# RWKV-7 scan norms by block-ones products with Ln and Exp, squares summed in pairs, and last weight chunks tile by tile, in a two-block transformer kernel on one core

## The chip, the cores and the metric

One core of one Trainium2 chip (trn2). The metric is the device time of one execution in microseconds (us); the time of a kernel is the median of several executions. TensorE, VectorE, ScalarE, GpSimd and SyncE run programs of their own and wait for each other by semaphores.

## The reference

256 tokens of width 2048 in fp32 go through two blocks. The first is an RWKV-7 mixer and a convolutional FFN, both with an adaptive modulation; the second is windowed attention beside HGRN2, and an MLP. Before and behind each of the four halves stands an RMS norm over all 2048 channels. What matters here, cut from the reference:

```python
def _rms(x, g):
    return x * lax.rsqrt(jnp.mean(x * x, axis=-1, keepdims=True) + 1e-6) * g
...
kk = heads(k * k_k)                       # 32 heads of 64 channels
kk = kk * lax.rsqrt(jnp.maximum(jnp.sum(kk * kk, axis=-1, keepdims=True), 1e-24))
...
y = _rwkv7_scan(rh, heads(decay), kh, vh, -kk, kk * ah)
mean = jnp.mean(y, axis=-1, keepdims=True)
var = jnp.mean(jnp.square(y - mean), axis=-1, keepdims=True)
y = (y - mean) * lax.rsqrt(var + 64e-5)
...
x = x + g_m * _rms(y, norm_mix_post)
h = _rms(x, norm_ffn_pre) * (1 + sc_f) + sh_f
f = _conv_ffn(h, ffn_w_in, ffn_conv_w, ffn_conv_b, ffn_w_out)
x = x + g_f * _rms(f, norm_ffn_post)
...
h = rmsnorm(x, mix_pre_gain_2)            # second block
x = x + rmsnorm(mixed, mix_post_gain_2)
x = x + rmsnorm(mlp(rmsnorm(x, mlp_pre_gain_2)), mlp_post_gain_2)
```

## The kernel before

**Layout.** Activations lie transposed: 16 tiles of 128 channels by 256 tokens. SyncE loads each weight in chunks (four k-tiles of 128 rows by up to 512 columns; the FFN's second product has chunks of two k-tiles) into a ring of raw slots. ScalarE copies a chunk into WH (L1208), VectorE subtracts that from the raw chunk into WL (L1715), three slots each, and both do so in the order of a fixed list of chunks; `walk(n)` brings an engine's part of that list up to chunk n. Activations are split into a high and a low half in the same way (XB). A product of a k-tile and an output tile is two matmuls: L779 over 512 columns (WH with both halves of the activations), L781 over 256 (WL with the high half).

**gemm() of TensorE (L760 to L790)** takes the output in groups of four tiles, each in a PSUM bank, and a group's weights chunk by chunk. In a chunk the k-tile is the outer loop and the output tile the inner one, so a group's four tiles end together behind the last k-tile of the last chunk. Each ended tile counts `s_tile`; ScalarE copies it out of the bank (L1270), or VectorE adds it to what is there (L1769, L1771), VectorE adds the low columns (L1762) and counts `s_ev`. `hook` calls other work in between.

**The RMS norms** have names: x and f before the first block's halves, o and f2 behind them, p, m, o2, m2 the same for the second block, at for attention's output. ScalarE squares a tile (`square`, L1211 to L1215, `s_sq`) into XX, a ring of three slots. TensorE adds it into bank 7 with a matmul by a 128x128 matrix of ones (`stat`, L741 to L748, `s_sqmm`), one matmul for each of 16 tiles. ScalarE takes the root (`root`, L1217 to L1220), VectorE the reciprocal (L1727 to L1729). For o, f2, o2 and m2 the squares of a group are made and summed beside the next group's chunks, two hooks a chunk; the last group's four come in `residual` (ScalarE L1240 to L1243) behind the gemm: for tiles 12 to 15 a square and a copy times the gain each, then the root. For p and m, whose norm is applied behind the product, a sum stands ahead of each k-tile of the first group. GpSimd does nothing in these stages but a few loads.

**prenorm("f")** (ScalarE L1295, VectorE L1856) makes the FFN's 16 input tiles: VectorE times the reciprocal root, ScalarE the modulation and the high half (into XB), VectorE the low half. The weight chunks whose slots are not free before are split behind it.

**The scan (447 to 878 us)** does the 32 heads in eight blocks of four heads (512 columns: four chunks of 64 tokens by two pairs of heads by 64). A round r holds `stage_t` of block r (six levels of 64x64 products on TensorE: L903, L913, L918, each followed by VectorE's TS L1986, WS L1979, QS L1990), `stage_s` of block r-1 (the state from chunk to chunk, TensorE L939 to L973, ScalarE's RS L1384, VectorE's UV L2005), and `side(r)`: the preparation of block b = r+1 and the end of block e = r-2. The three are generators, woven step by step by hand in the same order in each engine's program; where one engine waits, all steps behind stand too. `side` of all engines uses two PSUM banks, 6 and 7, in the order of the list ROUND (L526), a bank coming free when its READER (L528) has read it. In rounds 2, 4, 6, 8 a sixteen-instruction product of the modulation vector (L848) is in between, and VectorE accumulates other parts of it with L1698.

**The norms in side().** The keys' squares (kp) go through `head_sums` (L798: four matmuls with two columns of block ones each, giving 8 sums a token row), VectorE's maximum with 1e-24 into NS [128, 8], ScalarE's Sqrt (L1346), VectorE's reciprocal (L1899), `over_heads` (L803 to L809: eight matmuls of a broadcast column with the identity, spreading a value over its head's 64 rows; 16 instructions in the trace) and VectorE's product with kk (L1917). The output's squares (Y2) go the same way: VS, Sqrt (L1350), reciprocal (L1920), `over_heads`, product with y (L1941).

## Time and profile before

| | |
|---|---|
| median of the runs | 2953.48 us (3 runs, 2941.91 to 2957.41) |
| profiled execution | 2959.37 us, its span 2957.5 us |
| mean granted TensorE clock of the core | 0.963 of full speed |
| scan | 446.84 to 878 us; rounds 0 to 8 start at 446.84, 486.13, 528.21, 585.67, 634.34, 691.72, 740.39, 793.87, 832.67 |
| TensorE, weight load, VectorE, ScalarE, GpSimd busy | 95%, 80%, 63%, 43%, 3% |

A busy share is an average over the span. Engines in rows: PE is TensorE's matmul, PEld its weight load, DVE VectorE, ACT ScalarE, POOL GpSimd. In a timeline row the first number is the start in us from the span's start, the second the duration; in brackets stands the idle time of the engine before the instruction and what ended it. In a stretch the columns are its ends and length, the busy time (and count) of PE, PEld, DVE, ACT and POOL, the granted clock, the busy share of the DMA engines and their GB/s. A function table load of ScalarE is the row ACT_TABLE_LOAD.

### The profile page before, as it was taken

Reading aid. Unit: us, or ns where it says so; the run is one execution under the profiler, and the core shown is the slowest. Engines: PE = TensorE matmul, PEld = TensorE weight load, DVE = VectorE, ACT = ScalarE, POOL = GpSimd, SP = SyncE. Lnnn points to the kernel's source line nnn. Section 1 sums busy time; section 2 is a strip of 40 time slices with the busy share of each in tenths; the row PEclk is TensorE's granted clock in tenths of the full one; section 3 lists DMA queues with packets and bytes.
Section 4 is the critical chain, followed back from the end, with each engine's and each line's share of the span. In section 5 each row is a group of like instructions: output and inputs, shape, how many; then the busy total and the mean of one; then the engine's idle time right before and its main releaser. Section 6 shows DMA issues by size and latency. Waiting matters only on the chain.

```text
span 2957.5 us, 45793 instructions
## 1 busy us (share of the span) xinstructions
PE 2801.5 (95%) x19618; PEld 2374.6 (80%) x19618; DVE 1863.2 (63%) x2460; ACT 1281.7 (43%) x1735; POOL 102.6 (3%) x127
## 2 busy tenths in 40 slices
PE   6999988989879899999999989999999999999997
PEld 2488877778768688888888878888978888888886
DVE  3787647667644676766776756567656556565655
ACT  1244433332214555445445545466554444343443
POOL 0121001111000000000000000000000000000000
PEclk9999988889879899999999999999999999999999
DMA  9767732222316364866676545543445555555552
GB/s 385 260 233 238 255 125 80 101 86 83 105 58 207 107 192 148 294 199 196 236 243 194 172 156 163 170 144 100 132 139 181 189 185 179 191 185 182 186 189 85
DMA packets 289210, 514.11 MB, mean 174 GB/s; under 512 B 10096, under 2 KB 122736, under 8 KB 288880
## 3 DMA queue, kind: packets, MB, share of 16 engines
q1 hardware_dynamic: 286016, 500.21, 50.5%
q0 software_dynamic: 2560, 7.90, 0.8%
q8 instruction: 155, 2.54, 0.4%
q10 hardware_dynamic: 432, 3.07, 0.3%
q14 instruction: 47, 0.39, 0.0%
HBM read 508.91 MB, written 2.10 MB: 173 GB/s over the span
## 4 chain that ended last, share of the span: by engine, by line
PE 86%; DVE 5%; ACT 4%; issue 2%; DMA 2%; DVEq 0%; SPq 0%; POOL 0%; ACTq 0%
PE ps L779 46%; PE ps L781 23%; PE ps L745 2%; PE ps L918 2%; DMA RAWa<-in_ada_w 1%; PE ps L913 1%; PE ps L688 1%; PE ps L903 1%; PE ps L806 1%; ACT WHb L1208 1%; PE ps L1065 1%; PE ps L870 1%; PE ps L969 1%; PE ps L800 1%; PE ps L880 1%
## 5 line engine op out<-in xcount | busy, mean ns | idle before, releaser
L779 PE MATMUL ps<-XB,WHb 128*128 128x512 f32 x2304 | 833.6, 405 | 22.6 <-DVE WLb L1715 17.0
L781 PE MATMUL ps<-XB,WLb 128*128 128x256 f32 x2304 | 649.0, 282 | 0.0
L1715 DVE TENSOR_TENSOR WLb<-RAWb,WHb 128x2048 fp32r<-128x2048 f32 (+1 forms) x196 | 426.7, 2192 | 274.5 <-ACT WHb L1208 274.0
L779 PEld LDWEIGHTS ps<-XB,WHb 128*128 128x128 f32 x2304 | 437.0, 190 | 130.7 <-issue 18.3
L1208 ACT ACTIVATE WHb<-RAWb 128x2048 fp32r<-128x2048 f32 (+1 forms) x196 | 356.7, 1832 | 315.8 <-PE ps L781 279.4
L1715 DVE TENSOR_TENSOR WLd<-RAWd,WHd 128x2048 fp32r<-128x2048 f32 x144 | 328.2, 2289 | 253.2 <-ACT WHd L1208 253.2
L779 PE MATMUL ps<-XD,WHd 128*128 128x512 f32 x1280 | 460.0, 402 | 0.0
L781 PEld LDWEIGHTS ps<-XB,WLb 128*128 128x128 f32 x2304 | 439.3, 191 | 1.2
L1208 ACT ACTIVATE WHd<-RAWd 128x2048 fp32r<-128x2048 f32 x144 | 274.7, 1916 | 354.6 <-PE ps L781 354.6
L779 PE MATMUL ps<-FB,WHd 128*128 128x512 f32 x1024 | 364.5, 399 | 0.0
L781 PE MATMUL ps<-XD,WLd 128*128 128x256 f32 x1280 | 360.3, 281 | 0.0
L779 PEld LDWEIGHTS ps<-XD,WHd 128*128 128x128 f32 x1280 | 241.2, 188 | 59.1 <-DVE XD L1851 0.3
L781 PE MATMUL ps<-FB,WLd 128*128 128x256 f32 x1024 | 287.8, 281 | 0.0
L779 PE MATMUL ps<-XA,WHa 128*128 128x512 f32 x768 | 270.6, 398 | 1.7 <-DVE R L1762 1.7
L779 PE MATMUL ps<-FA,WHb 128*128 128x512 f32 x688 | 245.2, 401 | 0.4 <-DVE R L1762 0.4
L781 PEld LDWEIGHTS ps<-XD,WLd 128*128 128x128 f32 x1280 | 240.9, 188 | 0.7
L779 PEld LDWEIGHTS ps<-FB,WHd 128*128 128x128 f32 x1024 | 192.5, 188 | 47.4
L781 PE MATMUL ps<-XA,WLa 128*128 128x256 f32 x768 | 214.2, 279 | 0.0
L781 PE MATMUL ps<-FA,WLb 128*128 128x256 f32 x688 | 193.1, 281 | 0.0
L781 PEld LDWEIGHTS ps<-FB,WLd 128*128 128x128 f32 x1024 | 192.2, 188 | 0.3
L779 PEld LDWEIGHTS ps<-XA,WHa 128*128 128x128 f32 x768 | 144.2, 188 | 36.4 <-DVE R L1762 2.0
L779 PEld LDWEIGHTS ps<-FA,WHb 128*128 128x128 f32 x688 | 129.2, 188 | 32.2 <-DVE R L1762 0.7
(335 smaller groups left out, 3510.6 us busy)
## 6 DMA issues: line engine op xcount, KB each, us to landing
RAWb<-in_ffn_w_in SPq DMA_DIRECT2D x168, 512.0 KB, 5.1
RAWd<-in_w_up SPq DMA_DIRECT2D x64, 1024.0 KB, 5.2
RAWd<-in_w_down SPq DMA_DIRECT2D x64, 1024.0 KB, 5.1
RAWa<-in_ada_w SPq DMA_DIRECT2D x48, 1024.0 KB, 7.4
RAWa<-in_rwkv_w_rkv SPq DMA_DIRECT2D x48, 1024.0 KB, 5.6
RAWb<-in_ffn_w_out SPq DMA_DIRECT2D x36, 1024.0 KB, 5.5
RAWs<-in_ada_w SPq DMA_DIRECT2D x32, 1024.0 KB, 5.0
RAWb<-in_w_in SPq DMA_DIRECT2D x44, 512.0 KB, 5.0
```

The lines of the kernel that those rows point to most:

```text
L688: mm = pe.matmul(banks[ROW_BANKS[piece % 2][m]][0:1, :], SC[:, 2 * kc + 1:2 * kc + 2], RAW["a"][:, slot_of[i], 1024 + m * 512:1536 + m * 5 ...
L745: pe.matmul(banks[7][:, 0:T], ones, XX[:, (xx_at[stage] + j) % 3, :], start=(j == 0), stop=(j == n - 1), skip_group_check=True).then_inc(s ...
L779: pe.matmul(bank[:, :], WH[tag][:, w, o:o + P], acts(k), start=(k == 0), stop=False)
L781: mm = pe.matmul(bank[:, 0:T], WL[tag][:, w, o:o + P], acts(k)[:, 0:T], start=False, stop=last)
L800: mm = pe.matmul(bank[:, 2 * k:2 * k + 2], squares[:, k * P:(k + 1) * P], head2, start=True, stop=True)
L806: mm = pe.matmul(bank[64 * h:64 * h + 64, k * P:(k + 1) * P], rows[:, 2 * k + h:2 * k + h + 1].to_broadcast([P, 64]), ident, start=True, s ...
L870: mm = pe.matmul(bank[h][:, m * P:(m + 1) * P], BK[o, 4 * gg + m, :], AR[o, 4 * gg + m, :], start=True, stop=True)
L880: mm = pe.matmul(bank[:, i * T:(i + 1) * T], G2[:, k, i * P:(i + 1) * P], SG[:, k, :], start=(k == 0), stop=(k == 1))
L903: mm = pe.matmul(pair_at(pair_wt, m, u0), GM[rows, gm_index(m, u0), 0:64], istack[rows, :] if lv == 0 else TS[rows, m, :], start=True, sto ...
L918: mm = pe.matmul(pair_at(pair_q, m, u0), WS[rows, m, :], istack[rows, :] if lv == 0 else QS[rows, m, :], start=True, stop=True)
L1208: act.activation(WH[tag][:, n % WN, 0:size], RAW[tag][:, slot_of[i], 0:size], ACT.Copy).then_inc(s_wh, 1)
L1715: dve.tensor_tensor(WL[tag][:, n % WN, 0:size], RAW[tag][:, slot, 0:size], WH[tag][:, n % WN, 0:size].bitcast(F32), ALU.subtract).then_inc ...
```

## The change

1. Scan. Both norms' sums are one matmul over 512 columns with the 128x128 block ones (`blk`), which leaves in each row the sum of its head. For the keys VectorE takes the maximum with 1e-24 over 512 columns into sig, ScalarE Ln and then Exp with scale -0.5 (the inverse root), VectorE the product with kk. For the output ScalarE reads the bank with Ln (scale 1/64, bias a new constant eps_head), then Exp, VectorE the product with y. `head_sums`, `over_heads`, NS, VS, the two reciprocals and their steps and banks go. The maximum stands a step later in VectorE's order than before.
2. GpSimd adds the squares of two tiles (`pair_sums`), and `stat` is called for pairs: for tiles 0 to 11 in o, f2, o2, m2 and for all 16 in p, m.
3. In each gemm the last chunk of groups 1 and up has the output tile as the outer loop. ScalarE's `evac_to` makes squares of tiles 12 to 14 between its copies for o and o2; `residual` makes the squares first, then the root, then the four gain copies.
4. prenorm("f") calls `walk` for two weight chunks inside its loop: ScalarE ahead of tiles 8 and 12, VectorE behind tiles 10 and 14.

The diff, cut to its core:

```diff
-ROUND = [("a", "z"), ("a", "a"), ("e", "m1"), ("a", "n"), ("e", "v"), ("a", "nb"), ("p", "w"), ("e", "vb"), ("a", "bt0"),
+ROUND = [("a", "z"), ("a", "a"), ("e", "m1"), ("a", "n"), ("e", "v"), ("p", "w"), ("a", "bt0"),
          ("a", "bt1"), ("a", "g0"), ("a", "g1"), ("a", "g2"), ("a", "g3"), ("e", "g"), ("a", "bb"),
          ("a", "bv")]
-READER = {"z": (aA, "s1"), "a": (aA, "a1"), "n": (aV, "max"), "nb": (aV, "kkn"), "bt0": (aA, "bkt0"),
+READER = {"z": (aA, "s1"), "a": (aA, "a1"), "n": (aV, "max"), "bt0": (aA, "bkt0"),
           "bt1": (aA, "bkt1"), "g0": (aV, "gm0"), "g1": (aV, "gm1"), "g2": (aV, "gm2"), "g3": (aV, "gm3"),
-          "bb": (aV, "bo"), "bv": (aA, "uv1"), "m1": (zV, "mean"), "v": (zV, "var"), "vb": (zV, "nrm"),
+          "bb": (aV, "bo"), "bv": (aA, "uv1"), "m1": (zV, "mean"), "v": (zA, "lg"),
           "g": (zV, "out")}
...
-        pe.wait_ge(s_sq, sq_at[stage] + j + 1)
+        if j < n_pair[stage]:
+            pe.wait_ge(s_sp, pair_at_[stage] + j // 2 + 1)
+        else:
+            pe.wait_ge(s_sq, sq_at[stage] + j + 1)
         pe.matmul(banks[7][:, 0:T], ones, XX[:, (xx_at[stage] + j) % 3, :], start=(j == 0),
-                  stop=(j == n - 1), skip_group_check=True).then_inc(s_sqmm, 1)
-        if j == n - 1:
+                  stop=(j >= n - 2 if j < n_pair[stage] else j == n - 1),
+                  skip_group_check=True).then_inc(s_sqmm, 1)
+        if square_done(stage, j)[1] == sum_end[stage]:
             last7[0] = (s_rt, rms_no[stage] + 1)
...
-            if g and half:
-                stat(stage, 4 * g - 4 + ci, ND)
+            if g and half and ci % 2:
+                stat(stage, 4 * g - 5 + ci, ND)
...
-                for kk_, k in enumerate(ch["ks"]):
-                    if g == 0:
-                        if stage:
-                            stat(stage, k, ND)
-                        pe.wait_ge(*ready(k))
+
+                def product(kk_, k, t):
+                    i = gm.base[g] + t
+                    if k == 0 and tile_before[i] is not None:
+                        pe.wait_ge(s_ev, tile_before[i] + 1)
+                    o = kk_ * width + t * P
+                    bank = banks[tile_bank[i]]
+                    pe.matmul(bank[:, :], WH[tag][:, w, o:o + P], acts(k), start=(k == 0), stop=False)
+                    last = k == chunks[-1]["ks"][-1]
+                    mm = pe.matmul(bank[:, 0:T], WL[tag][:, w, o:o + P], acts(k)[:, 0:T],
+                                   start=False, stop=last)
+                    if last:
+                        mm.then_inc(s_tile, 1)
+                    return mm
+
+                full = len(ch["ks"]) == 4
+                if g and ch is chunks[-1]:
                     for t in range(nt):
-                        i = gm.base[g] + t
-                        if k == 0 and tile_before[i] is not None:
-                            pe.wait_ge(s_ev, tile_before[i] + 1)
-                        o = kk_ * width + t * P
-                        bank = banks[tile_bank[i]]
-                        pe.matmul(bank[:, :], WH[tag][:, w, o:o + P], acts(k), start=(k == 0), stop=False)
-                        last = k == chunks[-1]["ks"][-1]
-                        mm = pe.matmul(bank[:, 0:T], WL[tag][:, w, o:o + P], acts(k)[:, 0:T],
-                                       start=False, stop=last)
-                        if last:
-                            mm.then_inc(s_tile, 1)
-                    if hook and kk_ == 1 and len(ch["ks"]) == 4:
-                        hook(g, ci, 0)
+                        for kk_, k in enumerate(ch["ks"]):
+                            mm = product(kk_, k, t)
+                        if hook and t == nt // 2 - 1 and full:
+                            hook(g, ci, 0)
+                else:
+                    for kk_, k in enumerate(ch["ks"]):
+                        if g == 0:
+                            if stage and k % 2:
+                                stat(stage, k - 1, ND)
+                            pe.wait_ge(*ready(k))
+                        for t in range(nt):
+                            mm = product(kk_, k, t)
+                        if hook and kk_ == 1 and full:
+                            hook(g, ci, 0)
...
             pe.wait_ge(*aA(b, "sq"))
-            head_sums(take("a", b, "n"), kp[:, :]).then_inc(aP.sem, 1)
+            pe.matmul(take("a", b, "n")[:, :], blk, kp[:, :], start=True, stop=True).then_inc(aP.sem, 1)
...
             pe.wait_ge(*zA(e, "sq"))
-            head_sums(take("e", e, "v"), Y2).then_inc(zP.sem, 1)
-        if b is not None:
-            pe.wait_ge(*aV(b, "rec"))
-            over_heads(take("a", b, "nb"), NS).then_inc(aP.sem, 1)
+            pe.matmul(take("e", e, "v")[:, :], blk, Y2, start=True, stop=True).then_inc(zP.sem, 1)
         yield
...
-    def residual(stage, gm, n_pg):
+    def square_of(stage, gm, j):
+        act.wait_ge(s_ev, gm.tile0 + j + 1)
+        square(stage, j, R[:, j, :])
+
+    def residual(stage, gm, first):
+        for j in range(first, ND):
+            square_of(stage, gm, j)
+        root(stage)
         for j in range(12, ND):
-            squared(stage, gm, j, n_pg)
-        root(stage)
+            act.activation(R[:, j, :], R[:, j, :], ACT.Copy, scale=GB[:, j:j + 1]).then_inc(s_rs, 1)
...
-    def evac_to(dst):
+    def evac_to(dst, stage=None):
         def evac(gm, g):
             for t in range(n_tiles(gm, g)):
                 i = gm.base[g] + t
                 act.wait_ge(s_tile, i + 1)
                 act.activation(dst(gm, g, t), banks[tile_bank[i]][:, 0:T], ACT.Copy).then_inc(s_evh, 1)
+                if stage and g == 3 and t:
+                    square_of(stage, gm, 4 * g + t - 1)
...
-    def prenorm(stage, dst, scale, bias):
+    def prenorm(stage, dst, scale, bias, first):
         for j in range(ND):
+            if j in (8, 12):
+                walk(first + j // 4)
...
             act.wait_ge(*aV(b, "max"))
-            act.activation(NS[:, :], NS[:, :], ACT.Sqrt).then_inc(aA.sem, 1)
+            act.activation(sig[:, :], sig[:, :], ACT.Ln).then_inc(aA.sem, 1)
+            act.wait_ge(*aA(b, "lg"))
+            act.activation(sig[:, :], sig[:, :], ACT.Exp, scale=-0.5).then_inc(aA.sem, 1)
         yield
         if e is not None:
-            act.wait_ge(*zV(e, "var"))
-            act.activation(VS[:, :], VS[:, :], ACT.Sqrt).then_inc(zA.sem, 1)
+            act.wait_ge(*zP(e, "v"))
+            act.activation(Y2, e_bank(e, "v")[:, :], ACT.Ln, scale=1.0 / 64, bias=cst("eps_head")).then_inc(
+                zA.sem, 1)
+            act.wait_ge(*zA(e, "lg"))
+            act.activation(Y2, Y2, ACT.Exp, scale=-0.5).then_inc(zA.sem, 1)
         yield
...
             if j > 1:
                 lo(j - 2)
+            if j in (10, 14):
+                walk(first + j // 4)
...
-            dve.wait_ge(*aP(b, "n"))
-            dve.tensor_scalar(NS[:, :], a_bank(b, "n")[:, 0:8], 1e-24, None, ALU.max).then_inc(aV.sem, 1)
         yield
         if b is not None:
-            dve.wait_ge(*aA(b, "rt"))
-            dve.reciprocal(NS[:, :], NS[:, :]).then_inc(aV.sem, 1)
-        if e is not None:
-            dve.wait_ge(*zP(e, "v"))
-            dve.tensor_scalar(VS[:, :], e_bank(e, "v")[:, 0:8], 1.0 / 64, 64e-5, ALU.mult,
-                              ALU.add).then_inc(zV.sem, 1)
-        if b is not None:
+            dve.wait_ge(*aP(b, "n"))
+            dve.wait_ge(*aG(b, "pm"))
+            dve.tensor_scalar(sig[:, :], a_bank(b, "n")[:, :], 1e-24, None, ALU.max).then_inc(aV.sem, 1)
...
         if b is not None:
-            dve.wait_ge(*aP(b, "nb"))
-            dve.tensor_tensor(kk[:, :], kk[:, :], a_bank(b, "nb")[:, :], ALU.mult).then_inc(aV.sem, 1)
-        if e is not None:
-            dve.wait_ge(*zA(e, "rt"))
-            dve.reciprocal(VS[:, :], VS[:, :]).then_inc(zV.sem, 1)
+            dve.wait_ge(*aA(b, "rs"))
+            dve.tensor_tensor(kk[:, :], kk[:, :], sig[:, :], ALU.mult).then_inc(aV.sem, 1)
...
         if e is not None:
-            dve.wait_ge(*zP(e, "vb"))
-            dve.tensor_tensor(y, y, e_bank(e, "vb")[:, :], ALU.mult).then_inc(zV.sem, 1)
+            dve.wait_ge(*zA(e, "rs"))
+            dve.tensor_tensor(y, y, Y2, ALU.mult).then_inc(zV.sem, 1)
...
+    def pair_sums(stage):
+        for j in range(0, n_pair[stage], 2):
+            u = xx_at[stage] + j
+            pool.wait_ge(s_sq, sq_at[stage] + j + 2)
+            pool.tensor_tensor(XX[:, u % 3, :], XX[:, u % 3, :], XX[:, (u + 1) % 3, :],
+                               ALU.add).then_inc(s_sp, 1)
+
...
     pool.memset(UT[:, :, 0:2], 0.0).then_inc(s_utz, 1)
+    for stage in ("o", "f2", "p"):
+        pair_sums(stage)
     pool.wait_ge(s_xn, 2 * ND)
...
     pool.wait_ge(s_kd, 32)
+    for stage in ("o2", "m", "m2"):
+        pair_sums(stage)
```

`square_done(stage, j)` names the semaphore value at which square j has been read (by GpSimd's addition, `s_sp`, for the second of a pair; else by `stat`, `s_sqmm`); the list of XX's free slots is made from it. `n_pair` is 12 for o, f2, o2, m2, 16 for p and m, 0 for x, f, at.

## Rows read from the trace of the kernel before

**Rows 1.** The page's first part: busy time of TensorE, share of the span, instructions
```profile
PE 2801.5 (95%) x19618; PEld 2374.6 (80%) x19618; DVE 1863.2 (63%) x2460; ACT 1281.7 (43%) x1735; POOL 102.6 (3%) x127
```

**Rows 2.** Waits of TensorE's matmuls after the scan: total, times, longest
```profile
PE ps L779 <- DVE WLb L1715: 17.0, 3, 10.3
```

**Rows 3.** Stretches of scan rounds 2, 3 and 6: busy time by engine, granted clock, DMA
```profile
528.21:585.67 57.46, 51.58 (x789) 45.11 (x785) 35.94 (x63) 16.18 (x29) 6.63 (x8) 0.82 0.25 83
585.67:634.34 48.67, 44.31 (x773) 38.60 (x769) 36.34 (x62) 16.08 (x29) 7.71 (x8) 0.93 0.29 98
740.39:793.87 53.48, 47.59 (x788) 41.59 (x785) 35.94 (x63) 16.07 (x29) 5.59 (x6) 0.90 0.26 85
```

**Rows 4.** Timeline of TensorE in round 3: start, duration, [idle before, releaser]
```profile
590.13 1.10 PE L830 MATMUL ps<-MX,C 128*128 128x512 f32 x2 [0.78 <-ACT b L1319]
...
593.68 1.15 PE L903 MATMUL ps<-TS,GM 64*64 64x64 f32 x32
596.68 0.53 PE L963 MATMUL ps<-UV,BKT 128*64 128x64 f32 x8 [1.85 <-DVE UV L2005]
...
599.37 1.97 PE L806 MATMUL ps<-C,NS 128*64 128x128 f32 x16
...
605.43 1.15 PE L903 MATMUL ps<-TS,GM 64*64 64x64 f32 x32
...
609.46 1.15 PE L913 MATMUL ps<-WS,QS 64*64 64x64 f32 x32 [1.39 <-DVE WS L1979]
```

**Rows 5.** Timeline of ScalarE in round 3
```profile
591.99 0.63 ACT L1330 ACTIVATE XX<-MX 128x512 f32<-128x512 f32 x1 [0.87 <-DVE MX L1885]
...
596.67 1.28 ACT L1346 ACT_TABLE_LOAD   x1
```

**Rows 6.** Timeline of VectorE in round 3
```profile
600.32 0.68 DVE L1979 TENSOR_TENSOR WS<-ps,C 128x512 f32<-128x512 f32 x1
...
601.85 0.68 DVE L1917 TENSOR_TENSOR b<-b,ps 128x512 f32<-128x512 f32 x1
...
602.56 1.24 DVE L1698 SCALAR_TENSOR_TENSOR ACCs<-RAWs,SC,ACCs 128x1024 f32<-128x1024 f32 x1
```

**Rows 7.** The same work (level 2 to level 3) in rounds 2 and 6, as stretches
```profile
556.68:566.54 9.86, 9.86 (x125) 8.76 (x125) 5.06 (x10) 1.66 (x3) 0.00 (x0) 0.52 0.01 2
768.98:774.74 5.76, 5.76 (x125) 5.12 (x125) 5.06 (x10) 1.56 (x3) 0.00 (x0) 1.00 0.02 3
```

**Rows 8.** Timeline of ScalarE where it loads function tables, ahead of the scan
```profile
171.65 1.28 ACT L1284 ACT_TABLE_LOAD   x1
...
173.33 1.28 ACT L1285 ACT_TABLE_LOAD   x1
```

**Rows 9.** Chain of waits in the output projection: start, duration, one sum each
```profile
973.19 0.43 PE ps L745 x2
...
979.17 0.43 PE ps L745 x2
```

**Rows 10.** GpSimd's 128x256 adds: duration min, median, max
```profile
L2360 POOL TENSOR_TENSOR XX<-HV x48: 607/722/1594, 72.8 to 300.5; 128x256 f32<-128x256 f32 x48
```

**Rows 11.** Timeline of TensorE in the second block's input projection, first group
```profile
1774.72 0.59 PE L745 MATMUL ps<-XX,C 128*128 128x256 f32 x2
...
1776.55 0.59 PE L745 MATMUL ps<-XX,C 128*128 128x256 f32 x2
```

**Rows 12.** Timeline of TensorE where the FFN waits for a weight chunk
```profile
1025.95 0.50 PE L779 MATMUL ps<-XB,WHb 128*128 128x512 f32 x1 [4.05 <-DVE WLb L1715]
```

**Rows 13.** The stretch behind that wait: busy time, granted clock
```profile
1025.95:1031.30 5.35, 5.35 (x21) 4.64 (x22) 4.34 (x2) 1.22 (x1) 0.00 (x0) 0.68 0.81 252
```

**Rows 14.** Timelines of ScalarE at the square roots that end three projections
```profile
988.78 0.47 ACT L1219 ACTIVATE RST<-ps,C 128x256 f32<-128x256 f32 x1 [0.39 <-PE ps L745]
...
1762.27 0.47 ACT L1219 ACTIVATE RST<-ps,C 128x256 f32<-128x256 f32 x1
...
2941.66 0.47 ACT L1219 ACTIVATE RST<-ps,C 128x256 f32<-128x256 f32 x1 [0.39 <-PE ps L745]
```

92 lines of the change are left out of this document (46 added, 46 removed).

## The prediction

> **What bounds the kernel now.** I read the page first: TensorE is busy for 95% of the span [rows 1], so outside its idle stretches only less TensorE work shortens anything. Then the waits of TensorE behind the scan: there are few, and the largest that this change touches is for split weight chunks [rows 2]. Then the scan (447 to 878 us), stretch by stretch: there every round costs 48.7 us (rounds 3, 5), 53.5 (round 6) or 57.4 (rounds 2, 4), and the granted clock goes with it, 0.93, 0.90, 0.82 [rows 3]. One round at close range shows a chain of short steps over four engines [rows 4 to 6]: TensorE computes the level-1 product (L903, 593.68), then idles 1.85 us, and can go on with that level only at 601.0. What it waits for is VectorE's WS (L1979), which starts at 600.32 although its input was there at 594.8: VectorE executes in order, and ahead of WS stand the reciprocal of the keys' norms (waiting for a table load and Sqrt on ScalarE) and the output's sum (waiting for TensorE's eight two-column matmuls). At the end of this stretch TensorE waits again, 1.39 us, for the level-2 WS [rows 4]. Last, the clock: the same work, level 2 to level 3, takes 5.76 us at clock 1.00 and 9.86 us at 0.52 [rows 7], so a fall of the 2.4 GHz clock to 1.2 GHz there costs 4.1 us. It happened in rounds 2 and 4, behind an idle time of 2.06 us and one of 1.39; round 3, with only the 1.39, was spared.
>
> **Scan, keys' norms.** Per round go: 8 two-column instructions (1.05 us), the 16 of L806 (1.97 us at the low clock, [rows 4]), a Sqrt, a max and a reciprocal on 8 columns (0.2 each). Added: one 512-column product, 1.10 us as L830 [rows 4], so nothing is won at the sums themselves; a max over 512 columns, 0.68 as any VectorE operation of that size [rows 6]; Ln and Exp over 512 columns, 0.63 each [rows 5]. And table loads. Now a round has three, at Sigmoid, Exp and Sqrt, 1.28 us each. I count a load for each of Ln, Exp, Ln, Exp, six in a round, because of [rows 8]: Tanh and Sigmoid, one behind the other, each had their own load. The Trainium skill ("ScalarE activation tables", section Table sets in the compiler and the runtime) says that loads are placed by the greedy longest run of functions, and "ScalarE: Activation LUTs" (The hidden batching unit) that one set has both ln and exp and that Tanh is in Sigmoid's set. By that a round would have two loads; the trace, with two loads where that rule gives one, speaks against it.
>
> Replay of round 3 with the rows' durations. ScalarE is done with kp at 596.67 [rows 5]: load 1.28, Ln 0.63, load 1.28, Exp 0.63 give 600.5. VectorE has QS, UV by 595.95 (0.6 earlier, the 8-column max has left the step before), then max 596.6, AR 597.4, WS 598.0 instead of 601.0. TensorE: the state products 596.0 to 596.9, the output's sum to 598.0, level-1 products 598.1 to 600.1, U to 601.1. VectorE: kk 600.6 to 601.2, the accumulation (L1698, 1.24) to 602.5, TS 603.1. Level 2 starts at 603.2, was 605.43. Then QS, AR and two BK to 605.5, the output's product 606.1 (its Ln and Exp end at 604.4), WS 606.7; TensorE's next at 606.8, was 609.46: **2.65 us** earlier. Behind it the order is as before. GpSimd's product of kk waits for kk as before and is no later. RS (L1384) stands behind four ScalarE steps now and comes at 604.8, 0.7 earlier than before: no loss.
>
> In rounds 2, 4, 6 a vector of MOD is added between (L848, sixteen instructions). There level 2's second part starts 28.5 us after the round's start (556.68-528.21, 768.98-740.39, [rows 3, 7]) against 23.8 in round 3. By the replay it is 21.1 for round 3 and 1.1 more with L848 at the full clock: 22.2, **6.3 us** earlier.
>
> **The clock's price.** The replay leaves TensorE idle for 2.1, 0.6 and 1.4 us between 601.1 and 606.8, more than before in round 3, and the one stretch of before that looks like it (round 2) had the fall. So I charge 4.1 us [rows 7] to rounds 3, 5 and 6, which have no long fall now; rounds 2 and 4 have it already. Sum: 2x(2.65-4.1) + 2x6.3 + (6.3-4.1) = 11.9. Rounds 0, 1, 7, 8 have one L806 call each in front of the next product, 2.0 us [rows 4]: 8.0. Together **19.9 us**. Bounds: nothing won (loads eat all of it) and 19.9+20.5 = 40.4 (no fall in the five rounds).
>
> **Pair sums.** A sum over the tiles' squares takes 0.43 us of the path [rows 9]; in the gemms of "o", "f2", "o2", "m2" six each go: 24x0.43 = 10.3. GpSimd's add takes 0.72 (median, up to 1.59, [rows 10]) and lies beside a chunk of 5.98 us [rows 9]. Only f2's short chunks (two k-tiles) are too short for it: I charge 0.4 three times. 9.1. In the first groups of "p" and "m" TensorE is the bound too: 1.83 us from sum to sum [rows 11] is four tiles' products and one sum. Eight of 16 sums go in each: 16x0.43 = 6.9. The ring of three XX slots lets ScalarE run one tile less ahead, but at 1.4 us a step of TensorE that still covers a square (0.4) and an add. If GpSimd's adds take 1.59 each time, "p" and "m" win nothing: 6.9 is the term's bound below.
>
> **Last chunks tile by tile.** Tiles end 1.4 us apart instead of together. Of the tails, "o": the root at 988.78 [rows 14] waits for eight ScalarE operations in a row, of which four gain copies go behind the root, and the squares of tiles 12 to 14 before the end. New: last square at 986.4, the sums (five behind the gemm's end, 985.05) at 987.3: 1.45 us. "o2" is the same, 1.4. "f2" (root 1762.27, ahead of it a table load 1.28, which starts a gain copy and a tile's sum earlier) 1.45, "m2" (2941.66) 1.35, bounded by the five sums. **5.65**. Bound below: 0, when these sums run at the low clock. Between groups TensorE waits for no bank now, and the earlier evictions only help; same matmuls, same number.
>
> **Weight chunks inside "f".** TensorE waits 4.05 us for a chunk that ScalarE copies only behind all 16 prenorm tiles [rows 12], and the clock behind it is 0.68 for 5.35 us [rows 13]: at two levels that is 3.4 us at half, 1.7 lost. Moved ahead of tile 8, the chunk is split by about 1019.7, needed at 1021.9; the tiles behind it come 2 to 5 us later, but TensorE needs one only every 1.39. **5.75**; lower bound 1.7, if tile 12 comes late instead. No transfer starts otherwise: the DMAs of these chunks have landed, and SP's queue gets its slots no later. GpSimd's order changes too: its mask loads stand behind the "p" sums, some 2 us later, and are used a group later.
>
> **Sum.** 9.1+6.9+5.65+5.75 = 27.4 outside the scan, 19.9 in it: 47.3. The profiled execution took 2959.37 (span 2957.5), 5.9 above the median of the runs, 2953.48. So 2912.1 for that execution, and **2906 us** against the median.
>
> **The rivals.** (a) *The second fall stays away*: the 512-column products keep TensorE active. For it: rounds 3 and 5 have one fall only. Against: idle 4.1 of 5.7 us. 20.5 less: 2886. (b) *Fewer table loads*: Ln and Exp find their table loaded, two loads a round in place of six. kk at 597.9 instead of 600.5, 2.6 us less in each of 8 rounds, 20.8: 2885. (It is what the Trainium skill's rule above would give.) (c) *The scan wins nothing*: the four ScalarE operations and loads, 7.7 us a round for both norms, delay RS and the output's product. For it: ScalarE's order puts RS behind them. 2926. (d) *Slower*: in the middle of the round the clock stays low. All of round 3 behind 609.46, 24.9 us, at the factor 9.86/5.76 costs 17.7 us; in rounds 1 to 7 that is 124, less the 20.5 counted: about 3010. It decides above 8.9 us a round, half of that stretch. Against: in no round of before did a fall outlast the 128-column products. (e) *The change doesn't do what it says*: GpSimd becomes the wait of the sums in "p", "m" and the gemms. 16.0 less gain: 2922, which I take together with (c).
>
> **Chances.** Forecast 0.40, (a) 0.18, (b) 0.10, (c) and (e) 0.20, (d) 0.03; the rest, 0.09, lies between (c) and no change, from partly longer falls. One measurement of this kernel tells 0.5%, 14.8 us, from no change: faster 0.88, same 0.08, slower 0.04. Range: down to 2875 (most of (a) and (b)), up to 2938 ((c) and three further falls, 12.3).
>
> **What would show it.** In the profile of after: 0.43 us sums 40 fewer; the chunk wait of 4.05 gone; roots 1.4 earlier after the last product; in a middle round six table loads, kk about 15 us after the round's start; granted clock of rounds 3 and 5 below 0.93, of 6 at 0.82. A prediction of this size is wrong if rounds 3 and 5 are longer than 52 us, or if a round has two loads.

## The result, and the profile after

The kernel after takes **2927.05 us** (median of 7 runs, 2911.74 to 2932.53) against 2954.29 for the kernel before (7 runs, 2941.91 to 2959.64): ratio **0.991**, 95% interval 0.9894 to 0.9927, 27 us faster. Its profiled execution took 2927.05 (span 2925.2, granted clock 0.968), that of before 2959.37 (2957.5, 0.963): 32.3 us between the spans. I forecast 47.3 for the profiled execution and 2906 for the median. The experiments ran on four chips, each beside runs of the kernel before; their ratios are to those runs and compare the versions better than the medians do.

The page's first part, which answers to [rows 1]. TensorE has 45.5 us less to do, ScalarE 45 us more, GpSimd 79 more:

```profile
PE 2756.0 (94%) x19186; PEld 2322.3 (79%) x19186; DVE 1871.6 (64%) x2436; ACT 1326.6 (45%) x1776; POOL 181.8 (6%) x167
```

I read both traces at the same landmarks (the scan's first level-0 product, GpSimd's memory set behind the scan, the square roots of the norms, the first group's copies in the FFN, the first product of the FFN's and of the MLP's last part) and wrote down how the difference grows from each to the next. The last column is a second execution of the kernel after, described below, against the same execution of before:

| stretch | forecast | after | after, again |
|---|---|---|---|
| up to the scan | 0 | -2.3 | -5.0 |
| scan | -19.9 | -27.5 | -26.7 |
| output projection, to the root of o | -4.05 | -3.1 | -2.2 |
| prenorm f, to the first group's end | -5.75 | -6.0 | -6.1 |
| FFN, to its last part | 0 | +3.4 | -2.5 |
| that part, to the root of f2 | -2.85 | **+5.3** | +3.8 |
| to the root of p | -3.45 | **+1.3** | +1.2 |
| attention, HGRN2, to the root of o2 | -4.0 | -2.8 | -2.7 |
| to the root of m and the last part of the MLP | -3.45 | **+2.8** | +2.8 |
| to the root of m2 | -3.95 | -3.5 | -3.5 |

In these traces the scan won more than forecast and everything behind it next to nothing, 2.5 us. Both sizes hold for one pair of executions: against a second execution of the kernel before, described below too, the second one of the kernel after won 20.3 us in the scan and 6.8 behind it. In both pairs f2, p and m lost, and the scan won in other rounds than forecast. So there are two questions: why the middle of the kernel lost, and what won in the scan.

**The stalls in f2.** The list of TensorE's waits behind the scan (total, times, longest) has a new entry, three times 2.2 us for GpSimd's sums. The 4.05 us for a weight chunk of [rows 12] are gone; the two waits that stay under its name are the 13.2 us behind the scan, 10.3 before, and one of 2.6. The 13.2 us are no loss: TensorE's own last product of the scan ends earlier, and its next product starts 9.4 us behind the scan's end, 9.5 before.

```profile
PE ps L795 <- DVE WLb L1744: 15.7, 2, 13.2
PE ps L764 <- POOL XX L2389: 6.6, 3, 2.2
```

The timelines of GpSimd, VectorE and TensorE at the first of the three:

```profile
1676.60 2.53 POOL L2389 TENSOR_TENSOR XX<-XX 128x256 f32<-128x256 f32 x1 [11.11 <-ACT XX L1229]
```
```profile
1676.26 2.29 DVE L1744 TENSOR_TENSOR WLb<-RAWb,WHb 128x2048 fp32r<-128x2048 f32 x1 [0.41 <-ACT WHb L1222]
```
```profile
1679.19 0.70 PE L764 MATMUL ps<-XX,C 128*128 128x256 f32 x2 [2.15 <-POOL XX L2389]
...
1680.43 0.63 PE L795 MATMUL ps<-FA,WHb 128*128 128x512 f32 x1
```

GpSimd's addition has its two squares at 1676.5, but VectorE has begun to subtract a weight chunk 0.3 us earlier. The addition ends 0.6 us behind that subtraction: 2.53 us, where I had 0.72 from [rows 10]. Behind the stall the clock falls too (0.63 us for the 512-column product that takes 0.40 at the full clock). Over all 40 additions:

```profile
L2389 POOL TENSOR_TENSOR XX<-XX x40: 728/2275/2736, 891.7 to 2896.1; 128x256 f32<-128x256 f32 x40
```

**Round 3 of the scan**, which I had replayed. Here are its stretches and those of rounds 7 and 8 (the columns of [rows 3]; round 7 of before first, then after), and rows of TensorE, ScalarE and VectorE in round 3, which begins at 576.58:

```profile
793.87:832.67 38.80, 35.01 (x694) 31.29 (x691) 27.09 (x44) 4.04 (x9) 0.72 (x1) 0.91 0.36 117
832.67:878.81 46.14, 36.68 (x232) 28.69 (x230) 12.51 (x27) 6.59 (x15) 0.72 (x1) 0.63 0.02 6
```
```profile
576.60:624.90 48.30, 42.11 (x727) 35.27 (x725) 36.80 (x59) 22.02 (x34) 8.60 (x8) 0.93 0.30 99
...
778.60:811.81 33.21, 31.35 (x671) 27.17 (x669) 26.97 (x42) 7.68 (x12) 0.72 (x1) 1.00 0.41 137
811.81:849.09 37.28, 27.15 (x188) 18.83 (x186) 11.96 (x23) 13.84 (x21) 0.73 (x2) 0.80 0.03 8
```
```profile
594.98 1.97 PE L917 MATMUL ps<-TS,GM 64*64 64x64 f32 x32 [3.28 <-DVE TS L2008]
...
598.58 1.98 PE L927 MATMUL ps<-WS,QS 64*64 64x64 f32 x32 [0.79 <-DVE WS L2001]
```
```profile
588.54 1.28 ACT L1370 ACT_TABLE_LOAD   x1
...
590.48 1.28 ACT L1372 ACT_TABLE_LOAD   x1
...
592.42 1.28 ACT L1376 ACT_TABLE_LOAD   x1
...
594.42 1.28 ACT L1379 ACT_TABLE_LOAD   x1
```
```profile
592.43 0.69 DVE L1942 TENSOR_TENSOR b<-b 128x512 f32<-128x512 f32 x1 [2.09 <-ACT b L1372]
```

Each of Ln, Exp, Ln, Exp has its own table load, as I took from [rows 8]; the Trainium skill's rule of the greedy longest run ("ScalarE activation tables", Table sets in the compiler and the runtime) does not describe this program. kk's product starts 15.9 us after the round's start (forecast 14.9). Level 2 starts at 18.4 (forecast 17.5, before 19.8 by [rows 4]), behind an idle time of 3.28, and the next product at 22.0 (21.1; 23.8), 1.8 earlier than before. At level 2 the clock falls: 1.97 us for the product that took 1.15. The round ends up 0.4 us shorter. I had named the granted clock as a sign, below 0.93 in rounds 3 and 5 and 0.82 in round 6; it was 0.93, 0.87 and 0.87.

By rounds the scan went like this; the last column has the second execution of each kernel:

| rounds | before | after | forecast | measured | second executions |
|---|---|---|---|---|---|
| 0 and 1 | 39.3, 42.1 | 39.1, 43.5 | -4.0 | +1.2 | +3.6 |
| 2 and 4 | 57.5, 57.4 | 49.4, 51.4 | -12.6 | -14.1 | -10.8 |
| 3 and 5 | 48.7, 48.7 | 48.3, 50.9 | +2.9 | +1.9 | +2.0 |
| 6 | 53.5 | 51.4 | -2.2 | -2.1 | -2.0 |
| 7 and 8 | 84.9 | 70.5 | -4.0 | -14.4 | -13.1 |

### The profile page after: what moved, and what is told of

The parts are those of the page before. It is cut to its first block, busy times and chain, and to the rows that moved or that the text cites. A ratio compares the mean times of both kernels' runs of the same rounds, so it can differ in the third digit from the quotient of the medians.

```text
span 2925.2 us, 44978 instructions
## 1 busy us (share of the span) xinstructions
PE 2756.0 (94%) x19186; PEld 2322.3 (79%) x19186; DVE 1871.6 (64%) x2436; ACT 1326.6 (45%) x1776; POOL 181.8 (6%) x167
## 3 DMA queue, kind: packets, MB, share of 16 engines
q1 hardware_dynamic: 286016, 500.21, 51.1%
## 4 chain that ended last, share of the span: by engine, by line
PE 83%; DVE 6%; ACT 4%; issue 3%; DMA 2%; POOL 1%; DVEq 0%; SPq 0%; ACTq 0%
PE ps L795 46%; PE ps L797 23%; DMA RAWa<-in_ada_w 1%; PE ps L932 1%; PE ps L704 1%; PE ps L764 1%; PE ps L927 1%; PE ps L917 1%; ACT WHb L1222 1%; DVE WLb L1744 1%; PE ps L1079 1%; PE ps L884 1%; PE ps L734 1%; PE ps L983 1%; PE ps L894 1%
## 5 line engine op out<-in xcount | busy, mean ns | idle before, releaser
L2389 POOL TENSOR_TENSOR XX<-XX 128x256 f32<-128x256 f32 x40 | 74.4, 1861 | 1951.9 <-ACT XX L1229 1951.9
```

The source lines that it names most:

```text
L2389: pool.tensor_tensor(XX[:, u % 3, :], XX[:, u % 3, :], XX[:, (u + 1) % 3, :], ALU.add).then_inc(s_sp, 1)
```

## The experiments

### No pair sums where GpSimd's additions are slow

```diff
-n_pair = {..., "o": 12, "f2": 12, "p": 16, "o2": 12, "m": 16, "m2": 12}
+n_pair = {..., "o": 12, "f2": 0, "p": 0, "o2": 12, "m": 0, "m2": 12}
```

`stat` is called for single tiles there, as before.

> The kernel after, with no pair sums in f2, p and m (one sum for each tile there, as before); o, o2 and m2 keep them. Theory 1 (GpSimd's addition is the wait: it took 2.53 us beside VectorE's subtraction of weights, and TensorE stood 2.15 to 2.21 us three times in f2 and ran at the low clock behind it; in p and m two additions of 2.08 us stretched VectorE's low halves too, 1.34 us for two instead of 0.88): f2 gains the 5.3 us that it lost and 1.5 of the tail more, p and m 2.0 and 2.8 and perhaps 1 more each: 10 to 14 us faster than the kernel after, near 2914. Rival 2 (p, m and f2 lost time by the new order, squares before gain copies and tile-major chunks, not by the additions): within 3 us of the kernel after.

Measured: **2909.64 us**, ratio to the kernel before **0.9867** (0.9844 to 0.9889). The trace against that of before: f2 -1.4 instead of +5.3; p +0.6 instead of +1.3; m -0.3 instead of +2.8. So the pair sums of these three cost 6.7, 0.7 and 3.1 us, 10.5 in all, where I had counted a gain of 1.4, 3.45 and 3.45. Against the kernel after it is 12.7 us faster by the ratios, whose intervals lie apart, and 17 by the medians. The costs vary with the execution. f2 took 88.6 us in all three profiled executions without its pair sums, and 91.6 to 95.3 in the eight with them and the new chunk order, so they cost 3.0 to 6.7; in m it is 1.9 to 3.2, in p 0.1 to 0.8. And p stays 0.3 to 1.1 us longer than in the kernel before without them, so a little of rival 2 is left.

In p two mechanisms can be read; what each costs was not tried. A square of a new tile waits until TensorE has summed a pair, since XX has three slots, and ScalarE's weight chunk stands behind that square; and the additions stretch VectorE's low halves. GpSimd's, VectorE's and TensorE's rows at the first stall of p, in the kernel after:

```profile
1745.75 2.08 POOL L2389 TENSOR_TENSOR XX<-XX 128x256 f32<-128x256 f32 x1 [2.52 <-ACT XX L1229]
```
```profile
1744.96 2.29 DVE L1744 TENSOR_TENSOR WLb<-RAWb,WHb 128x2048 fp32r<-128x2048 f32 x1 [2.73 <-ACT WHb L1222]
1747.17 1.34 DVE L1880 SCALAR_TENSOR_TENSOR XB<-X,V,XB 128x256 fp32r<-128x256 f32 x2
```
```profile
1748.26 0.47 PE L795 MATMUL ps<-XB,WHb 128*128 128x512 f32 x1 [1.63 <-DVE XB L1880]
```

The two low halves took 0.88 us in the kernel before. I had argued that a step of 1.4 us covers a square and an addition, and had not looked at what stands behind the square on ScalarE.

### The last chunks with the k-tile outside

```diff
-if g and ch is chunks[-1]:
+if False:
```

> The kernel after with the k-tile as the outer loop in the last chunks too; the squares ahead of the root and the gain copies behind it stay. Theory (tiles that end one by one let three of the last four squares run ahead of the end): each of the four tails is 0.7 to 1.3 us longer, 3 to 5 us slower in all; the three stalls of 2.2 us in f2 go or shrink, since the last chunk's additions stand elsewhere, or stay as they are if only the square's time sets them. Rival (the order of root and gain copies alone was the gain of the tails): within 1 us.

Measured: 2918.39 us, ratio 0.9891 (0.9867 to 0.9916). The theory held for the tails of o and m2 (0.8 and 0.9 us longer; of o two executions of one kernel differ as much), not for o2 (0.0). The total is not slower: 9 us below the kernel after by the medians, 5.6 by the ratios. f2 explains 6 of them: -0.9 us instead of +5.3, with all pair sums in place. Its timelines of GpSimd, VectorE and TensorE at the same point:

```profile
1672.06 0.73 POOL L2389 TENSOR_TENSOR XX<-XX 128x256 f32<-128x256 f32 x1 [11.11 <-ACT XX L1229]
```
```profile
1672.27 2.66 DVE L1744 TENSOR_TENSOR WLb<-RAWb,WHb 128x2048 fp32r<-128x2048 f32 x1
```
```profile
1672.84 0.70 PE L764 MATMUL ps<-XX,C 128*128 128x256 f32 x2 [0.35 <-POOL XX L2389]
```

This is the clearest pair of rows in the study. Here VectorE is held up by the accumulation of a tile that ends late, and so the addition starts first, by 0.21 us: it takes 0.73, and VectorE's subtraction 2.66 instead of 2.29. In the kernel after tiles end one by one, VectorE is free earlier, the subtraction starts first, and the addition takes 2.53. The two exclude each other, and the first to start goes first. The small stall that I had charged to f2 (0.4, three times) is the 0.35 here; that the other edit would turn it into 2.2 I had not seen. The Trainium skill ("SBUF — State Buffer", SBUF: two separate sides) states such a rule: the two engines share a pair of ports that is locked for a whole instruction, by a VectorE operation with two SBUF inputs (against a GpSimd operation that reads SBUF) or by the GpSimd operation, whichever starts first. The rows agree with it, and I had not weighed it in the prediction. Counted over the kernel after from both timelines, 27 of the 40 additions begin while VectorE subtracts a chunk and take 1.4 to 2.7 us, and the seven that begin beside an idle VectorE take 0.7.

### No pair sums at all

```diff
-n_pair = {..., "o": 12, "f2": 12, "p": 16, "o2": 12, "m": 16, "m2": 12}
+n_pair = {..., "o": 0, "f2": 0, "p": 0, "o2": 0, "m": 0, "m2": 0}
```

> The kernel after with no pair sums at all. Beside the run without pairs in f2, p and m it puts twelve single sums back into each of o and o2 and leaves the tail of m2 without pairs. Theory (each of six sums saved in o, o2 and m2 is worth 0.43 us of TensorE, nothing hides it): 2.6 us longer in each of the three stages, 7.7 in all than the run without slow pairs, so near 2917. Rival (the pair's sum waits for GpSimd there too, and wins nothing): within 2 us of it, stage by stage.

Measured: 2919.81 us, ratio 0.9883 (0.9857 to 0.991), near the 2917 of the theory. Against the first experiment o, o2 and m2 are 2.0, 1.5 and 2.4 us longer: 5.9 for 18 sums, 0.3 each, where I had 0.43 each (o is the uncertain one, since the two executions of the kernel before differ by 1.5 us in it). The additions take 2.5 us there too, but beside a chunk of 5.65 they are hidden. With no pairs the run also shows the tails alone: -1.1, -1.3, -1.0, -1.0 us for o, f2, o2, m2 against the kernel before; I had 1.45, 1.45, 1.4, 1.35.

### The weight chunks behind the prenorm again

```diff
-                    if j in (8, 12):
-                        walk(first + j // 4)
...
-                    if j in (10, 14):
-                        walk(first + j // 4)
```

> The kernel after with the two weight chunks split behind the 16 tiles of the prenorm again. Theory: TensorE's wait of 4 us at the FFN's start is back, and the low clock behind it: the first group ends 5.7 us later, and all behind it too. Rival (the wait moves: TensorE was held by the prenorm's last tiles anyway): under 2 us.

Measured: 2923.09 us, ratio 0.9904 (0.9884 to 0.9924). In the trace the stall is back to the hundredth, and the first group ends 5.7 us later than in the kernel after:

```profile
995.89 0.50 PE L795 MATMUL ps<-XB,WHb 128*128 128x512 f32 x1 [4.05 <-DVE WLb L1742]
```

The median does not show it: it is 4 us below that of the kernel after, 1.8 by the ratios. A part of 5.7 us is smaller than what separates two executions, so this part is shown by the trace alone.

### The norms of the scan, one by one and both

The two-column sums, the Sqrt, the reciprocal and the spreading come back for one norm or for both; the diffs are the change's own lines, reversed.

> The kernel after, with the keys' norm as before, the output's norm new. Theory 1: rounds 7 and 8 take 70 us; rounds 2 and 4 are back at 57 us, so 10 to 14 us slower than the kernel after. Rival 2 (the wait for table loads of the keys' Ln and Exp eats their gain): within 3 us of the kernel after or faster.

> The kernel after, with the output's norm as before (two-column sums, Sqrt, reciprocal, spreading over heads), the keys' norm new. Theory 1 (each norm works for itself; from round 7 on only the output's is in the round): rounds 7 and 8 take 84 to 85 us as before instead of 70.5, rounds 2 and 4 keep most of their gain of 8.1 and 6.0: some 12 to 16 us slower than the kernel after. Rival 2 (the time is in the clock, which falls by chance of phase): rounds 7 and 8 stay near 70 us.

> The kernel after, with both norms as before; the pair sums, the tile-major chunks and the chunks inside the prenorm stay. Theory: the scan takes 432 us instead of 404.5 and the whole is 27 us slower than the kernel after, so within 3 us of the kernel before, since the other parts together won nothing (2.6 us in the traces). Rival (my forecast: the other parts are worth 27.4): 27 us faster than the kernel before.

| | median | ratio | rounds 0 to 6 | rounds 7, 8 | scan |
|---|---|---|---|---|---|
| after | 2927.05 | 0.991 | 39.1, 43.5, 49.4, 48.3, 51.4, 50.9, 51.4 | 70.5 | 404.5 |
| output's norm new | 2923.62 | 0.9908 (0.9883 to 0.9932) | 39.9, 42.4, 51.2, 46.4, 51.8, 48.0, 51.4 | 70.3 | 401.4 |
| keys' norm new | 2949.13 | 0.9987 (0.9969 to 1.0004) | 38.4, 43.2, 56.1, 54.6, 54.6, 51.0, 51.8 | 80.1 | 429.9 |
| both old | 2944.48 | 0.998 (0.9962 to 0.9998) | 39.9, 42.3, 54.2, 48.7, 57.4, 48.6, 53.5 | 83.6 | 428.2 |

**The output's norm is the whole gain**, and the keys' norm is worth nothing. My theory of two independent gains fell. Over all profiled executions the scan took 399.6 to 405.9 us with both norms new (seven, one with another order of the logarithms), 401.4 and 404.4 with the output's alone, 429.9 with the keys' alone, and 425.6 to 432.0 with both old (three). With the output's norm alone round 3 takes 46.4 us at clock 0.96, the shortest middle round of the study:

```profile
580.41:626.82 46.41, 41.83 (x751) 34.97 (x747) 36.08 (x60) 19.78 (x32) 7.65 (x8) 0.96 0.31 103
```

Why the keys' norm wins nothing can be read at level 2 of round 3. With the output's norm alone, kk's product starts 15.4 us after the round's start and level 2 at 18.3; with both new it is 15.9 and 18.4. The larger maximum, two table loads, Ln and Exp thus take no less time here than the small maximum, one load, Sqrt, the reciprocal and the spreading. But the spreading (L842) stood where TensorE has nothing else to do. Without it TensorE idles for 3.28 us in front of level 2, and from there to level 3 it runs at granted clock 0.65 for 9.72 us, where it took 7.87 at 1.00. Rows with the output's norm alone, then that stretch in it, then in the kernel after:

```profile
594.50 1.24 PE L842 MATMUL ps<-C,NS 128*64 128x128 f32 x16
...
598.73 1.15 PE L936 MATMUL ps<-TS,GM 64*64 64x64 f32 x32
```
```profile
595.79 0.69 DVE L1960 TENSOR_TENSOR b<-b,ps 128x512 f32<-128x512 f32 x1 [0.25 <-PE ps L842]
```
```profile
598.73:606.60 7.87, 6.27 (x134) 5.58 (x132) 7.60 (x14) 1.73 (x4) 1.12 (x3) 1.00 0.40 134
```
```profile
594.98:604.70 9.72, 8.94 (x133) 8.17 (x134) 8.66 (x16) 2.99 (x6) 1.51 (x3) 0.65 0.33 110
```

In rounds 2, 4 and 6 the keys' norm does bring level 2 forward, from 21.3 us to 19.1, and the way to level 3 is longer there too: 10.1, 11.8 and 11.8 us for 9.7, 10.3 and 9.9.

Another part stands on GpSimd. In round 3 of before, its subtraction for pm (L2381) began 0.57 us ahead of VectorE's small maximum NS and the accumulation behind that, and took 1.27 us (the accumulation 1.69 for 1.24); in the kernel after the keys' maximum stands a step later, VectorE goes straight on to the accumulation, and the same subtraction starts behind its start and takes 2.22. ScalarE's Exp waits for it, and all of ScalarE's chain behind is 0.9 us later; that is the 0.9 by which my replay missed at kk, level 2 and the next product. It is so in all profiled executions: with the keys' norm as before the subtraction takes 1.27 in rounds 1 to 6, with it new 2.2 in the odd rounds and 1.7 in the even ones. The kernel before first, then the kernel after:

```profile
593.22 1.27 POOL L2381 TENSOR_TENSOR b<-b 128x512 f32<-128x512 f32 x1 [2.52 <-DVE b L1892]
```
```profile
584.13 2.22 POOL L2410 TENSOR_TENSOR b<-b 128x512 f32<-128x512 f32 x1 [2.52 <-DVE b L1923]
```

The last run, both norms old, says what the rest of the change was worth: 8.5 us by the medians (2952.96 for the kernel before beside it), 5.9 by the ratio, with an interval that ends at 0.9998, where I had 27.4. Its theory (nothing) and its rival (27.4) were both off.

What the output's norm wins in rounds 7 and 8 stands in VectorE's order. VectorE's rows and TensorE's in round 8 of before, then TensorE's of after:

```profile
837.89 0.17 DVE L1902 TENSOR_SCALAR VS<-ps 128x8 f32<-128x8 f32 x1 [1.76 <-PE ps L800]
837.97 0.28 DVE L2016 COPY STA<-ps 128x128 f32<-128x128 f32 x1
838.36 0.43 DVE L2019 TENSOR_TENSOR SD<-STA,DM 128x256 f32<-128x256 f32 x1
```
```profile
838.84 0.43 PE L939 MATMUL ps<-SD,AR 128*64 128x128 f32 x2 [0.98 <-DVE SD L2019]
...
840.38 3.57 PE L848 MATMUL ps<-C,ACCs 128*128 128x1 f32 x16
```
```profile
816.99 0.43 PE L953 MATMUL ps<-SD,AR 128*64 128x128 f32 x2
...
818.03 1.95 PE L865 MATMUL ps<-C,ACCs 128*128 128x1 f32 x16
```

The state's SD stands behind VS, which waits for TensorE's sums. Without VS, SD is ready in time, TensorE does not idle for 0.98 us, and the clock does not fall there: the sixteen instructions of MOD take 1.95 us instead of 3.57. In all four profiled executions with the output's norm as before they took 3.57 or 3.58, in all ten with it new 1.94 or 1.95, the version with Sqrt (next) among them. The spreading (1.97) and an idle 1.11 behind it go as well. In round 7 the granted clock is 1.00 for 0.91; of the 5.6 us won there 3.7 are less busy time and 1.9 less idle time.

### Sqrt and reciprocal for the output

```diff
-act.activation(Y2, e_bank(e, "v")[:, :], ACT.Ln, scale=1.0 / 64, bias=cst("eps_head"))
...
-act.activation(Y2, Y2, ACT.Exp, scale=-0.5)
+act.activation(Y2, e_bank(e, "v")[:, :], ACT.Sqrt, scale=1.0 / 64, bias=cst("eps_head"))
...
+dve.reciprocal(Y2, Y2)
...
 dve.tensor_tensor(y, y, Y2, ALU.mult)
```

> The kernel after; the output's norm keeps its one block-ones product, but its inverse root is ScalarE's Sqrt over 512 columns and VectorE's reciprocal over 512 columns (256 columns took 1.75 us, so an estimate of 3.5) in place of Ln and Exp. It has one table load less on this way (1.28) and one ScalarE operation less (0.63), and 3.5 us more on VectorE, in whose order TensorE's next operands stand. Theory 1 (what the output's norm wins is TensorE's second trip, 16 spreading instructions and their wait): rounds 7 and 8 stay below 75 us, and the middle rounds lose 1 to 3 us each by the reciprocal, 5 to 18 us slower than the kernel after in all. Rival 2 (Ln and Exp are the gain): rounds 7 and 8 are back at 80 us or more, 20 us or more slower.

Measured: 2946.13 us, ratio 0.9968 (0.9953 to 0.9983), 19 slower than the kernel after, 17 by the ratios. Each of rounds 2 to 6 is 3.3 to 3.4 us longer (52.7, 51.7, 54.7, 54.3, 54.8), just over the top of theory 1, and rounds 7 and 8 take 78.1, between the two theories. The reciprocal:

```profile
L1961 DVE RECIPROCAL XX<-XX x8: 3336/3344/3354, 550.2 to 868.3; 128x512 f32<-128x512 f32 x8
```

Its 3.34 us come back one for one in rounds 2 to 6: here what stands in VectorE's order is on the path, what ScalarE does for the same value is not. So Ln and Exp are needed for the gain, because they take a reciprocal that became 512 columns wide off VectorE.

### Both logarithms together

```diff
 act.activation(sig[:, :], sig[:, :], ACT.Ln)
-act.wait_ge(*aA(b, "lg"))
-act.activation(sig[:, :], sig[:, :], ACT.Exp, scale=-0.5)
...
 act.activation(Y2, e_bank(e, "v")[:, :], ACT.Ln, scale=1.0 / 64, bias=cst("eps_head"))
...
+act.wait_ge(*aA(b, "lg"))
+act.activation(sig[:, :], sig[:, :], ACT.Exp, scale=-0.5)
...
 act.wait_ge(*zA(e, "lg"))
 act.activation(Y2, Y2, ACT.Exp, scale=-0.5)
```

> The kernel after with ScalarE's order Ln (keys), Ln (output), Exp (keys), Exp (output) in place of Ln, Exp, Ln, Exp: the same work, four table loads in a middle round in place of six. Theory 1 (the loads of 1.28 us stand on the way to kk and y): the output's values come 2.6 us earlier, but the keys' Exp waits for the output's sum on TensorE, a step later; where the one makes good for the other the middle rounds are 0 to 2 us shorter each, 0 to 10 us in all. Rival 2 (the keys' Exp is what VectorE waits for, so its delay of a step counts and the saved loads do not): rounds 2 to 6 are 1 to 3 us longer each, 5 to 15 us slower. In rounds 7 and 8 nothing changes by either.

Measured: 2923.19 us, ratio 0.9907 (0.9884 to 0.9929); rounds 2 to 6 take 49.3, 48.9, 51.1, 51.4, 51.0 against 49.4, 48.3, 51.4, 50.9, 51.4. Two loads of 1.28 us a round are gone (ScalarE's busy time in a middle round is 19.4 for 22.1), and the time is the same. The saved loads and the later Exp of the keys cancel, as the theory allowed: level 2 starts 0.4 us earlier in the even rounds and 0.7 later in the odd ones. What the loads cost when nothing else moves was not tried.

### The output's norm alone, and no slow pairs

> The kernel after with the keys' norm as before (as in the run with the output's norm only) and without the pair sums of f2, p and m. Theory 1 (the gain of the scan is the output's norm alone, and the slow pairs are a loss of their own; the two add up): 0 to 4 us faster than the run without slow pairs (2909.64), so 2905 to 2910, and 13 to 18 faster than the run with the output's norm only (2923.62). Rival 2 (one of the two readings was the difference of two executions): 2915 or more.

Measured: 2914.27 us (2905.94 to 2918.96), ratio 0.9866 (0.9844 to 0.9888), the same as with the keys' norm new. The median lies between the 2910 of theory 1 and the 2915 of its rival; against the run with the output's norm only it is 9 us faster, not 13. Both versions without slow pairs beat both kernels, by 13 to 17 us (the kernel after) and 39 (the kernel before, by the ratios).

### Both kernels once more

> The kernel before, unchanged, one more profiled execution. Its FFN's first product took 5.493 us from chunk to chunk where the kernel after took 5.600, with the same matmuls at the same granted clock; over runs of one and the same FFN code both values came up. Theory 1 (the pace of an unbroken row of matmuls differs from execution to execution): here some of the stretches at 5.49, 5.65 and 5.58 change their value, while the scan's rounds agree within 1 us. Rival 2 (it belongs to the program): all the same to 0.01.

> The kernel after, unchanged, one more profiled execution. Rounds 4 and 5 of the scan took 51.4 and 50.9 us there, and 49.8 and 48.6 in the run with the last chunks by k, whose scan code is the same. Theory 1 (a fall of the clock more or less, by execution): rounds 0 to 3, 6 and the last two within 0.5 us of the first execution, rounds 4 and 5 at one of these two values; the stalls of f2 (2.15 to 2.21 us, three) are there to 0.1 us. Rival 2 (the start of the scan, which the rest of the program moves, decides): rounds 4 and 5 as in the first execution.

Measured: 2953.88 and 2918.53 us. In the kernel before the three stretches kept their pace to 0.01, as the rival has it, but the rounds did not agree within 1 us: round 0 took 37.3 us for 39.3, round 2 54.2 for 57.5, the last two 83.6 for 84.9, and the whole scan 425.6 for 432.0. In the kernel after the scan repeated (405.3 for 404.5; rounds 4 and 5 again 51.4 and 50.9, so 49.8 and 48.6 did not come by chance of an execution: the run without any pairs has them too. These are also the two of this scan code that start their scan latest, at 449.9 and 449.1 us where the others start between 441.8 and 446.0, which speaks for the rival; what decides it stays open). The three stalls of f2 are there again, 2.15, 2.15 and 2.20. But the pace of the FFN's first product changed. Both kernels' profiled executions in 88 us of unbroken matmuls, the kernel after first, then before, then the kernel after again:

```profile
1036.00:1124.00 88.00, 88.00 (x499) 76.29 (x499) 60.54 (x80) 47.93 (x64) 0.00 (x0) 1.00 0.55 176
```
```profile
1074.00:1162.00 88.00, 88.00 (x509) 77.00 (x508) 62.64 (x80) 48.54 (x65) 0.00 (x0) 1.00 0.56 177
```
```profile
1034.00:1122.00 88.00, 88.00 (x509) 76.95 (x508) 61.78 (x81) 48.52 (x65) 0.00 (x0) 1.00 0.56 178
```

At the granted clock 1.00 and with TensorE busy throughout, the same program issues 499 matmuls in one execution and 509 in the other. It is not the chip alone: of the fourteen profiled executions six have the slower pace in this stretch and eight the faster, and three chips show both. 3.1 of the +3.4 us of the first table lie in this product; in the second execution it took 0.9 us less than in the kernel before: no part of the change.

## Why the prediction was right, and where it was not

The sign, the range (2875 to 2938) and the replay of the middle rounds held; which of the two norms gives the gain, and what the pair sums cost, did not. By its own steps:

- **Table loads, six a round.** Right. Rival (b), fewer loads, did not come.
- **Replay of round 3 and the clock's price.** Right within 0.9 us: level 2 1.4 us earlier than before, the next product 1.8 (forecast 2.65), in rounds 2, 4 and 6 5.8 to 5.9 (forecast 6.3). The fall of the clock came, so rival (a) did not; I had charged 4.1 for it in rounds 3, 5 and 6, and by the rounds' ends it cost 1.4, 4.0 and 3.8. The rounds 2 to 6 gave 14.3 where the sum had 11.9, and 10.8 between the second executions. What was missing is that GpSimd's subtraction takes longer when VectorE's order closes up.
- **"Rounds 0, 1, 7, 8 have one L806 call each, 2.0 us".** This step failed, both ways. In rounds 0 and 1, which have only the keys' norm, the scan got 1.2 us slower (3.6 between the second executions). In rounds 7 and 8, which have only the output's, it got 14.4 faster (13.1): I counted the spreading and not the wait of SD behind VS, nor the falls of the clock that these waits caused.
- **Keys' and output's norm as one gain.** I costed the keys' path in detail and gave the gain of rounds 2 to 6 to both. The runs give it all to the output's: the keys' new way brings kk no earlier in an odd round, and the spreading that it saves stood in time that TensorE now idles.
- **Pair sums.** This term was mis-sized. The duration of GpSimd's addition was taken from subtractions of its size that mostly ran beside short VectorE operations or none, 0.72 (the 1.59 were four beside its accumulation over 1024 columns); its median here is 2.275. In o, o2 and m2 it is hidden (5.9 us won for 7.7 forecast). In f2, p and m it is not: 10.5 us of cost where I had 8.3 of gain. This is rival (e), GpSimd becomes the wait, which I had put into one case with (c) and valued at 16.0 us less gain; it was 21.
- **Tails.** Right in kind, 4.4 us for 5.65. The chunk order has 0.8 of it in o, 0.9 in m2 and nothing in o2; by that the rest lies with the squares and the root ahead of the gain copies, which was not tried alone.
- **Weight chunks inside f.** Right: 5.7 for 5.75.

The middle case thus did not come as summed: the scan gave 7.6 us more than forecast, the rest 25 less (27.4 forecast, 2.5 measured; 3.4 went to the pace). Between the second executions it is 0.4 more and 20.6 less. That the scan's sum lies so near is luck: 9 to 10 us too little for rounds 7 and 8 stand against 5 to 8 too much for rounds 0 and 1. The median, 27 us for the forecast's 47, lies beside rival (c), 2926, but not by its mechanism: (c) had the scan win nothing.

## What to carry to other kernels

Take the duration of a helper engine's instruction from rows where the neighbour is doing what it will be doing, not from its quiet ones: an addition put at 0.72 us took 2.3 beside a stream of weight subtractions, and which of the two started first decided whether TensorE waited 0.35 or 2.2 us. When a value's way crosses several engines, price first what it makes the in-order engine hold back (the small sum VS, 0.17 us long, held SD up for a microsecond, and the clock fell behind it), and only then its own length. Ask of work taken off TensorE whether it stood in an idle time: the keys' spreading did, and taking it away won nothing. And cost an edit in every round that has it alone; the rounds with only one norm would have told the two apart.

## What the runs showed of the hardware that was not expected

- The size of this was not expected: GpSimd's addition (SBUF to SBUF, fp32, 128x256) and VectorE's subtraction of a weight chunk exclude each other: 0.73 and 2.66 us when the addition starts first, 2.53 and 2.29 when the subtraction does. Beside VectorE's accumulation from PSUM (L1800) three additions of the run with the last chunks by k took 0.73. GpSimd's subtraction over 512 columns took 1.27 when it began before VectorE's accumulation over 1024, and 2.22 when it began 0.16 us behind it.
- An unbroken row of matmuls at granted clock 1.00 has two paces, 499 or 509 matmuls in 88 us (2%), and one program shows either from execution to execution. With the clock's falls in the scan (425.6 or 432.0 us for the kernel before) this is why differences under 6 us were read from stages and not from medians.
- Four table loads a round or six changed a round by 0.6 us at most, up or down, although ScalarE was 2.7 us busier with six. With four, one Exp stood later, so this is no price of a load alone.
